# Attention's side work at other places: seventh query tile, the sixth tile's copies, retention turns and their copies, and the second compressed scores

## What is computed

```
h = rms_norm(x, ln_mix_pre[l])
proj = h @ w_in[l]
rq, rk, rv, rg, nq, nkv, ngate = jnp.split(proj, bounds, axis=-1)
y_ret = retention(rq, rk, rv, rg)
y_nsa = nsa(nq, nkv, ngate, ...)
mix = jnp.concatenate([y_ret, y_nsa], axis=-1) @ w_out[l]
x = x + rms_norm(mix, ln_mix_post[l])
```

## Time and profile before

| | us |
|---|---|
| median of 3 runs | 1400.08 |
| lowest and highest | 1399.67 and 1400.54 |
| the profiled execution | 1401.01 |
| its span (first to last instruction) | 1399.1 |
| PE busy | 1363.3 (97%) |
| DVE, ACT, POOL busy | 713.3, 606.3, 700.1 |

### The profile page before, as it was taken

One profiled execution on the slowest core, in us unless ns is written; L12 is line 12 of the kernel. 1 busy time (PEld: TensorE's weight loads), 2 busy tenths in 40 slices (PEclk: granted clock), 3 DMA queues, 4 the chain that ended last, 5 costly groups with the idle time before them and its releaser, 6 DMA issues.

```text
span 1399.1 us, 17721 instructions
## 1 busy us (share of the span) xinstructions
PE 1363.3 (97%) x6904; PEld 1122.8 (80%) x6904; DVE 713.3 (51%) x900; ACT 606.3 (43%) x1087; POOL 700.1 (50%) x544
## 2 busy tenths in 40 slices
PE   8999988999999999999999999989999999999998
PEld 5889866778888888888888887767788888888886
DVE  5406556745544544644462075566355445556443
ACT  4233565756434333433442336656454333343322
POOL 2544775745444444544464456757435444445441
PEclk9999998999999999999999999989999999999999
DMA  5433420022333333333233333100323333333231
GB/s 202 136 100 106 131 65 16 1 91 91 105 91 97 99 93 103 90 103 93 61 121 112 108 106 119 31 16 2 121 68 115 104 91 104 93 96 100 90 106 61
DMA packets 34883, 127.19 MB, mean 91 GB/s; under 512 B 3952, under 2 KB 4464, under 8 KB 34416
## 3 DMA queue, kind: packets, MB, share of 16 engines
q1 hardware_dynamic: 34656, 125.53, 29.2%
q10 hardware_dynamic: 144, 0.52, 0.1%
HBM read 123.94 MB, written 2.10 MB: 90 GB/s over the span
## 4 chain that ended last, share of the span: by engine, by line
PE 89%; ACT 5%; DVE 3%; issue 1%; POOL 1%; DMA 0%; DVEq 0%; POOLq 0%; ACTq 0%; SPq 0%
PE bank L1719 33%; PE bank L1372 17%; PE bank L1751 17%; PE bank L1388 5%; PE bank L1616 3%; PE bank L1654 2%; PE bank L1677 2%; PE bank L1678 1%; ACT E L813 1%; PE bank L1562 1%; PE bank L1563 1%; PE bank L1476 1%; PE bank L1583 1%; PE bank L1340 1%; POOL w_lo L546 1%
## 5 line engine op out<-in xcount | busy, mean ns | idle before, releaser
L546 POOL TENSOR_TENSOR w_lo<-raw,w_hi 128x1024 fp32r<-128x1024 f32 x216 | 521.3, 2419 | 468.4 <-ACT w_hi L643 468.1
L643 ACT ACTIVATE w_hi<-raw 128x1024 fp32r<-128x1024 f32 x220 | 230.9, 1054 | 241.9 <-DMA raw<-wstream 241.8
L1719 PE MATMUL bank<-act_hi,w_hi 128*128 128x512 f32 (+1 forms) x768 | 286.0, 372 | 0.6 <-DVE act_lo L926 0.6
L1719 PE MATMUL bank<-act_hi,w_lo 128*128 128x512 f32 (+1 forms) x768 | 285.2, 371 | 0.0
L1719 PE MATMUL bank<-act_lo,w_hi 128*128 128x512 f32 (+1 forms) x768 | 285.2, 371 | 0.0
L885 ACT ACTIVATE cv<-bank,par 128x512 f32<-128x512 f32 x88 | 68.6, 779 | 286.0 <-PE bank L1719 286.0
L1301 DVE SCALAR_TENSOR_TENSOR cv<-bank,par,cv 128x511 f32<-128x511 f32 x88 | 66.0, 750 | 225.3 <-ACT cv L885 225.3
L1719 PEld LDWEIGHTS bank<-act_hi,w_hi 128*128 128x128 f32 x768 | 144.7, 188 | 26.9 <-DVE act_lo L926 1.6
L1719 PEld LDWEIGHTS bank<-act_hi,w_lo 128*128 128x128 f32 x768 | 144.7, 188 | 25.2
L1719 PEld LDWEIGHTS bank<-act_lo,w_hi 128*128 128x128 f32 x768 | 144.7, 188 | 24.7
L1372 PE MATMUL bank<-w_hi,act_hi 128*128 128x512 f32 (+1 forms) x384 | 144.5, 376 | 0.6 <-DVE w_lo L926 0.5
(11 more groups left out here) (175 smaller groups left out, 2231.9 us busy)
## 6 DMA issues: line engine op xcount, KB each, us to landing
raw<-wstream SPq DMA_DIRECT2D x220, 512.0 KB, 3.6
g_all<-gains SPq DMA_DIRECT2D x2, 2048.0 KB, 7.0
x_out<-x SPq DMA_DIRECT2D x8, 256.0 KB, 2.0
x<-x_in SPq DMA_DIRECT2D x3, 512.0 KB, 9.3
const<-consts SPq DMA_DIRECT2D x1, 1030.0 KB, 13.7
g_all<-gains ACTq DMA_DIRECT2D x1, 512.0 KB, 5.1
x<-x_in SPq DMA_DIRECT2D x2, 256.0 KB, 5.2
par<-pars SPq DMA_DIRECT2D x2, 235.0 KB, 3.5
```

What stands on the lines that cost most here:

```text
L546: nc.gpsimd.tensor_tensor(w_lo[:, s, :], raw_slot(s), r32(w_hi[:, s, :]), ALU.subtract)\
L643: nc.scalar.activation(w_hi[:, s, :], raw_slot(s), ACT.Copy).then_inc(hi_ready, 1)
L1719: last = mm(bank[:, b, first:end], a, v, start=(k == 0 and n == 0), stop=(k == KD - 1 and n == 2), skip_group_check=True)
```

## The change

Five things move; no arithmetic is added or taken away.
- Tile 6's copies on ACT go behind the last two early jobs, and its rests on DVE behind `compressed_first(0)`.
- Tile 7's steps go from items 1 to 8 to items 2 to 8, with two steps at item 6. Its copies stay at item 9.
- The retention turns go from items 9, 11, 13, 15 to 10, 13, 16, 19. The first waits for tile 6's rests only. The copy to `act_hi` is made by ACT at the turn's own item (`y_round`), the rest by DVE an item later (`y_rest`).
- The compressed scores of group 1 go from items 18 to 21 to items 20 to 23, and `compressed_first(1)` from item 22 to item 24. The first piece of the output projection stays at item 24.
- The scores of unit 7 go from item 10 to item 9.

```diff
-        CMP_BANK, CMP_AT = (7, 0), (0, 22)
-        Q7_AT = 1
-        Y_AT = (9, 11, 13, 15)
+        CMP_BANK, CMP_AT = (7, 0), (0, 24)
+        Q7_AT = {2: (0, 1), 3: (1, 2), 4: (2, 3), 5: (3, 4), 6: (4, 6), 7: (6, 7), 8: (7, KD)}
+        Q7_END = 9
+        Y_AT = (10, 13, 16, 19)
...
-        UNIT_SCORES = {4: (3, 4), 5: (5, 6), 6: (7,), 7: (10,), 8: (11, 12, 13, 14), 9: (15, 16, 17, 18),
+        UNIT_SCORES = {4: (3, 4), 5: (5, 6), 6: (7,), 7: (9,), 8: (11, 12, 13, 14), 9: (15, 16, 17, 18),
...
+                def y_round(n):
+                    act.wait_ge(y_turned, upto(y_turned, l, n + 1))
+                    nc.scalar.activation(act_hi[:, 0:4, n * P:(n + 1) * P],
+                                         bank[:, 0, :].rearrange("p (k c) -> p k c", k=4), ACT.Copy).then_inc(y_h, 1)
...
-                    if z == 13:
-                        queries_first(6)
+                queries_first(6)
...
-                    if k == Q7_AT + 8:
+                    if k == Q7_END:
                         queries_first(7)
+                    if k in Y_AT:
+                        y_round(Y_AT.index(k))
...
-                def y_round(n):
-                    dve.wait_ge(y_turned, upto(y_turned, l, n + 1))
-                    nc.vector.tensor_copy(act_hi[:, 0:4, n * P:(n + 1) * P],
-                                          bank[:, 0, :].rearrange("p (k c) -> p k c", k=4)).then_inc(y_h, 1)
+                def y_rest(n):
                     dve.wait_ge(y_h, upto(y_h, l, n + 1))
...
-                    if z == 14:
-                        queries_rest(6)
                 compressed_first(0)
+                queries_rest(6)
...
                     if k - 1 in Y_AT:
-                        y_round(Y_AT.index(k - 1))
+                        y_rest(Y_AT.index(k - 1))
...
-                        pe.wait_ge(q_l, upto(q_l, l, 8))
+                        pe.wait_ge(q_l, upto(q_l, l, 6))
...
-                    if Q7_AT <= k < Q7_AT + KD:
-                        if k == Q7_AT:
+                    if k in Q7_AT:
+                        if k == min(Q7_AT):
                             pe.wait_ge(c_step, upto(c_step, l, 3))
-                        feature_tile(l, 7, range(k - Q7_AT, k - Q7_AT + 1))
+                        feature_tile(l, 7, range(*Q7_AT[k]))
```

## The result

The changed kernel takes 1409.82 us (median of 6 runs, 1406.46 to 1413.47) against 1400.16 before (6 runs, 1399.67 to 1400.78): ratio 1.0072, 95% interval 1.0061 to 1.0083. It is slower, by 9.7 us, and it scatters over 7 us where the kernel before scattered over 1 (over 4 in 24 later executions). The forecast was 1398.0 and the range ended at 1404.5. The profiled execution has a span of 1407.9 (1399.1 before).

What follows compares the result with a forecast made beforehand. PE, busy 97% of the span, was taken as the bound, so only its gaps and clock could give time. Terms of −8 us and +6 for the clock behind new waits gave −2: 1398.0 us, range 1391.5 to 1404.5.

Steps and rivals of the forecast that it cites:

- item 9 to its product: From item 9's turn to its product, 10.35 us becomes 4.8, −5.5 a layer, with about 1.0 of waiting left.
- item 20's wait: New wait of the compressed scores for the last retention rest: +2.9 us a layer (2.3 to 3.6).
- item 24's: New wait: the projection comes later because compressed_first(1) follows item 24's rest, +2.7 us a layer (2.3 to 3.0).
- waits between items 11 and 19 within the 0.7: Items 11 to 19: short waits on `pt_l` from ACT's bunched work, +0.7 us a layer (0 to +2).
- Item 2's turn: Items 1 and 2: PE idles unbroken, 3.5 us, before item 2's turn; net +0.3 a layer (0 to +1.0).
- The sum without the new clock: All terms except the clock behind the new waits: −8 us for both layers.
- I take 3.5 short spells: +6: Clock behind four new waits at items 20 and 24: 3.5 spells of 3.4 us at half clock, +6 in total.
- Long spells behind item 20: Rival, chance 0.22: 6.8 to 9.75 us at half clock behind item 20's wait; total +1.5 to +7, middle 1404.
- two of the six places: Items 2, 20 and 24 in both layers; slower than before once more than two give a spell above 3.4 us.
- the clock stays up: Rival, chance 0.22: no lower clock behind most new waits; total −8 us (−10 to −5), 1392.
- ACT's taking over of the copies: Items 11 to 19: four copies of 0.59 us a layer added to ACT, +0.7 a layer (0 to +2).
- the gain from DVE's copy: Items 11 to 19: turns three apart and DVE's copy gone remove waits and a slow-clock spell, −4.8 us a layer.

Runs made afterwards that it cites:

- run 3: Changed kernel with group 1's compressed scores replaced by four 128x512 bf16 matmuls an item, waits at items 20 and 24 kept: 1403.91 us.
- run 4: Changed kernel with group 1's compressed scores replaced by 128x512 bf16 matmuls and the first projection piece at item 26, item 20's wait kept: 1392.99 us.
- run 2: Changed kernel with the first output projection piece at item 26 instead of 24, item 20's wait kept: 1404.18 us.
- run 6: Changed kernel with compressed scores at items 22 to 25, read at 26, projection from 28, PE still waiting at item 20: 1402.62 us.
- run 8: Changed kernel with turns at items 10, 12, 14, 16, compressed scores at 18 to 21, read at 22, tile 7's steps at 1 to 8: 1386.29 us.
- run 9: run 8 with the retention copies back on DVE, ahead of the rest: 1392.00 us.
- run 10: Kernel before with turns at items 10, 12, 14, 16, the first waiting for tile 6 only, and unit 7's scores at item 9: 1393.41 us.
- run 11: run 8 with tile 6's copies and rests in their old places: 1386.15 us.
- run 1: Changed kernel with retention turns at items 10, 12, 14, 16 instead of 10, 13, 16, 19, item 24's wait kept: 1398.76 us.

## Why the prediction was wrong

**The waits and their sizes: right.** The reasoning that priced them from rows of before held to 0.5 us: item 9 to its product 4.8 expected, 4.81 measured; item 20's wait 2.9 and 2.88; item 24's +2.7 (in delay) and 2.79 and 2.39 (in idle); items 2 to 9 0.7 longer (17.07 against 16.4 before); waits between items 11 and 19 within the 0.7. Item 2's turn came 0.3 earlier, at 204.90, behind an idle of 3.2 (3.5 expected), and the product of item 9 waited 0.5 where I had 1.0.

**The sum without the new clock: right.** I had −8; the growth of the span, 8.8, less the 17.3 lost in new spells gives −8.5.

**The step that failed** is the term "I take 3.5 short spells: +6". Measured: behind item 20 spells of 13.6 and 23.9 us, the second over item 24's wait as well, and none behind item 24 in layer 0; together 17.3 us lost. I had taken the shortest spell of the rows (3.4, behind a wait of 2.0) as likeliest for waits that lay between 2.0 and 3.6, and interpolated by the length of the wait. Runs 3 and 4 show that the length of the wait doesn't set the length of the spell: at the same 2.9 it is 3.4 with the wide stand-ins behind it. Nor does the length of a wait say whether a spell comes at all. The trace of before has an idle of 3.23 near its start, longer than the waits at items 20 and 24, which my rows left out and at which the clock held:

```profile
6.10:9.30 3.20, 0.00 (x0) 0.01 (x1) 0.88 (x2) 1.95 (x5) 0.95 (x3) 1.00 1.03 415
9.35:20.00 10.65, 9.84 (x47) 6.68 (x48) 8.18 (x11) 7.90 (x15) 2.31 (x6) 1.00 1.03 414
```

**The rival was right in kind and too small.** "Long spells behind item 20", over narrow pieces, is what happened, and I gave it 0.22. I bounded a spell by the longest seen (9.75), so the case ended at +7 and the range at 1404.5. There was no reason for such a bound. The stretch of narrow pieces in the new order is four items long, about 8 us at the full clock and 14 at half (run 2), and the spells of 13.6 (changed kernel) and 17.0 (run 2) in layer 0 lasted about that long. In layer 1 the spell went on into item 24's wait and its projection. The case was also added up too low by its own terms: 1.7 to 3.2 more a layer behind item 20 and "up to as much again" behind item 2 is up to 12.8 for both layers, so it reached +10.8, 1411, and not +7; and two of the six places with a spell of 6.8 are enough to bring −2 above zero, not more than two.

**The rival "the clock stays up"** didn't come about in the changed kernel. In all ten profiled layers with a wait of 2.8 to 2.9 at item 20 the clock fell, within 0.8 us of the end of the wait or (run 2, layer 1) 5.8 us later. The Trainium skill, "TensorE: Matmul & The Clock Gate", section "Why this matters for your kernels", allows pauses of that length; these ten layers disagree, item 24's wait of 2.79 in layer 0 agrees, and so, by its time and mean clock, does the fastest execution of run 6. So what failed is the rival's "most of the new waits", and such waits are not safe.

**Two smaller misses.** I counted ACT's taking over of the copies as a cost of up to 2 us a layer, beside the gain from DVE's copy that I had put into the waits. With turns two items apart, runs 8 to 11 show the two together as a gain of 5.7 and 7.3 for both layers, with the waits on `act_lo` going from 7.7 to 3.6, because DVE's copy stood in the chain from a turn to the next; with turns three apart no run shows what it is worth. And the longer spell behind item 2's unbroken idle didn't come in the changed kernel (3.4 in both layers, a mean clock of 0.90 as before), but a spell of 6.8 did stand there in one layer each of runs 1 and 4, so that it stayed away was luck in part.

## What stays open

Behind item 24's wait there was no spell in layer 0 of the changed kernel, one of 3.4 in some layers and one of 10.2 in others (run 1 layer 1, run 3 layer 0), over 128x512 work and ordinary items, with no 128x32 piece. So narrow pieces are not needed for a long spell; what else decides its length wasn't found. That it is their width that makes a spell long isn't shown either, since the stand-ins of runs 3 and 4 differ in type and operands too: float32 stand-ins of 128x512 would tell. With one trace for each kernel, some of the differences between layers may be chance. Nor was it tried whether a filler of matmuls in place of the wait would hold the clock: all eight banks are in use at item 20.

## What to carry to other kernels

When a wait of the matrix engine moves, look at what stands behind it: the same pause of 2.9 us cost 1.7 us of clock in all four layers with the 128x512 bf16 stand-ins behind it, and 6.7 to 10.5 in three of four with the 128x32 ones, 1.7 in the fourth. Put the producer of a side result two items ahead of its consumer rather than in the same item, and a copy on the engine that is not in the chain to the next turn. When a forecast rests on the length of something whose cause isn't known, don't bound it by the longest one seen; here the scatter of the runs (7 to 20 us in the changed kernel and runs 2 and 6, against 1 to 4 in the kernels with neither wait) shows how free it was.

## What the runs showed of the hardware

Spells at the lower clock level (0.50) lasted from 3.4 us to 23.9 us, the longest while PE was busy for 21.1 of them; in run 2 PE was busy without a pause through all 17.0. Idle times of 3.2 (the start of the kernel before) and 2.8 (item 24, layer 0 of the changed kernel) were followed by no spell, and idle times of 1.3 (run 9) by spells of 6.8 and 3.4. Two layers with the same instructions and the same wait had spells of 13.4 and 3.4 (run 6) and of 17.0 and 3.4 (run 2). The short one of run 2 began 5.8 us behind the wait, inside narrow matmuls that ran without a pause.
